# One stationary block for the rounded values and their rest in the 64-column heads, and the two halves of the bank added afterwards

## What is computed

```python
o_a = _diff_attention(a_q, a_k, a_v, ...)        # 4 heads, values 128 wide, then a norm per head
o_b = _forgetting_attention(b_q, b_k, b_v, ...)  # 8 heads, values 64 wide
o_c = _stick_breaking_attention(c_q, c_k, c_v)   # 8 heads, values 64 wide
m = (gates[:, :, 0] * (o_a @ proj_a[l])
     + gates[:, :, 1] * (o_b @ proj_b[l])
     + gates[:, :, 2] * (o_c @ proj_c[l]))
h = h + m @ w_out[l]
```

## Time and profile before

| | us |
|---|---|
| executions | 2615.31, 2614.27, 2615.72 |
| median | 2615.31 |
| profiled execution, device time | 2615.27 |
| its span | 2613.5 |
| TensorE busy | 2579.9 |
| VectorE busy | 1429.5 |
| ScalarE busy | 1104.7 |
| granted TensorE clock | 0.998 of full speed |

### The profile page before, as it was taken

The page is one execution under the profiler, slowest core; times in us unless marked ns, Lnnn a source line. Parts: engine busy times, 40 slices in busy tenths (PEclk is TensorE's granted clock), DMA queues, the critical chain, the costliest instruction groups (busy, mean ns, idle before and its releaser), DMA issues.

```text
span 2613.5 us, 37200 instructions
## 1 busy us (share of the span) xinstructions
PE 2579.9 (99%) x11966; PEld 2142.6 (82%) x11966; DVE 1429.5 (55%) x2260; ACT 1104.7 (42%) x1856; POOL 7.0 (0%) x13
## 2 busy tenths in 40 slices
PE   7999999999999999999999999999999999999998
PEld 6888888888888888888888888888888888888886
DVE  5444347788854464444344443477787455544434
ACT  4333237776632243332233322477776223433322
POOL 0000000000000000000000000000000000000000
PEclk9999999999999999999999999999999999999999
DMA  4222331111122232222332222211111222322232
GB/s 166 96 96 97 103 106 57 65 58 57 57 90 97 95 113 96 96 96 102 108 105 96 96 97 105 89 65 60 62 57 57 100 93 95 115 96 96 97 105 104
DMA packets 65769, 238.07 MB, mean 91 GB/s; under 512 B 7296, under 2 KB 7552, under 8 KB 65408
## 3 DMA queue, kind: packets, MB, share of 16 engines
q1 hardware_dynamic: 65664, 236.79, 26.0%
HBM read 234.66 MB, written 2.10 MB: 91 GB/s over the span
## 4 chain that ended last, share of the span: by engine, by line
PE 91%; DVE 4%; ACT 2%; issue 2%; DMA 0%; DVEq 0%; ACTq 0%; SPq 0%
PE ps L372 29%; PE ps L374 28%; PE ps L373 28%; PE ps L504 2%; ACT area L738 2%; DVE stat L1166 1%; DVE w_lo L1030 1%; PE ps L454 1%; DVE area L1030 1%; PE ps L443 0%; PE ps L445 0%; PE ps L491 0%; PE ps L493 0%; DVE area L1160 0%; DVE scratch L1046 0%
## 5 line engine op out<-in xcount | busy, mean ns | idle before, releaser
L738 ACT ACTIVATE w_hi<-w_raw 128x1024 fp32r<-128x1024 f32 x441 | 468.6, 1063 | 1161.1 <-PE ps L374 1160.2
L372 PE MATMUL ps<-u_hi,w_hi 128*128 128x512 f32 x2368 | 928.6, 392 | 13.9 <-DVE w_lo L1030 13.5
L374 PE MATMUL ps<-u_hi,w_lo 128*128 128x512 f32 x2368 | 923.0, 390 | 0.0
L373 PE MATMUL ps<-u_lo,w_hi 128*128 128x512 f32 x2368 | 922.9, 390 | 0.0
L1030 DVE TENSOR_TENSOR w_lo<-w_raw,w_hi 128x1024 fp32r<-128x1024 f32 x441 | 538.9, 1222 | 313.8 <-ACT w_hi L738 305.7
L372 PEld LDWEIGHTS ps<-u_hi,w_hi 128*128 128x128 f32 x2368 | 445.2, 188 | 105.7 <-issue 13.1
L374 PEld LDWEIGHTS ps<-u_hi,w_lo 128*128 128x128 f32 x2368 | 445.1, 188 | 93.8
L373 PEld LDWEIGHTS ps<-u_lo,w_hi 128*128 128x128 f32 x2368 | 445.4, 188 | 90.8 <-issue 1.0
L372 PE MATMUL ps<-area,w_hi 128*128 128x512 f32 x1024 | 398.8, 389 | 0.4 <-DVE h L1050 0.4
L374 PE MATMUL ps<-area,w_lo 128*128 128x512 f32 x1024 | 398.4, 389 | 0.0
L373 PE MATMUL ps<-area,w_hi 128*128 128x512 f32 x1024 | 398.4, 389 | 0.0
(11 more groups left out here) (112 smaller groups left out, 1621.8 us busy)
## 6 DMA issues: line engine op xcount, KB each, us to landing
w_raw<-weights SPq DMA_DIRECT2D x441, 512.0 KB, 3.2
h<-x SPq DMA_DIRECT2D x2, 1024.0 KB, 7.3
out<-scratch SPq DMA_DIRECT2D x8, 256.0 KB, 2.2
scratch<-const_b SPq DMA_DIRECT2D x1, 512.0 KB, 10.7
scratch<-const_r SPq DMA_DIRECT2D x1, 320.0 KB, 10.3
scratch<-lambdas SPq DMA_DIRECT2D x1, 256.0 KB, 11.3
cst<-const SPq DMA_DIRECT2D x1, 137.0 KB, 2.2
par<-params SPq DMA_DIRECT2D x1, 94.0 KB, 2.0
```

Source lines behind the costliest of these rows:

```text
L372: pe.matmul(dst, hi, x_hi, start=start, stop=False, **kw)
L373: pe.matmul(dst, hi, x_lo, start=False, stop=False, **kw)
L374: return pe.matmul(dst, lo, x_hi, start=False, stop=stop, **kw)
L738: return act.activation(dst, src, ACT.Copy)
```

## The change

The values of a 64-column head are put into one block of 128 columns: head 0's rounded values on columns 0 to 63 and their rest on 64 to 127, head 1's the other way round. `val(branch, hd)` is now such a pair of one head, not a part of both; there are no zeros, and `v_area` shrinks from 4096 to 3072 columns, with GpSimd's fill and the wait for it gone. A head's sum is two matmuls per block of keys (with the rounded and with the rest weights), both with the same stationary block. The product of the two rests is in it now, which was left out before. Half of the bank then holds what the rounded values give, the other half what their rest gives, and the two have to be added:

- `output_rest(hd)` on ScalarE copies the half of the rest, across the partitions, into `o_rest` at the head's own half;
- `output_whole(hd)` on VectorE adds the bank's other half to it, into `o_whole`;
- `output_hi` and `output_lo` of these branches read `o_whole` (SBUF), not the bank.

Each head is an accumulation group of its own, so the bank is free for the next one only when `output_whole` of the last has run; the TensorE waits for that (`o_whole_set`) ahead of each sum. `weighted_whole` keeps the three matmuls for the differential branch. In the stick-breaking output's place `values_hi(1)` and `values_lo(1)` with `rows` now go ahead of `output_hi(2, t)` and `output_lo(2, t, layer)`.

```diff
@@ val, val_block
-            at = j * P if branch == 0 else j * 3 * HEAD + head * HEAD
-            return val(branch, part)[:, at:at + P]
+        def val_block(branch, part, j):
+            return val(branch, part)[:, j * P:(j + 1) * P]
...
-            pool.memset(v_area[:].bitcast(F32), 0.0).then_inc(zeros_set, 1)
...
+            def weighted(branch, hd):
+                for j in range(NQ):
+                    pe.wait_ge(pt_set, c.next(pt_set))
+                    n, w_hi_j, w_lo_j = wide_keys(j)
+                    v = val_block(branch, hd, j)
+                    pe.matmul(ps[:, OB, SEQ - n:SEQ], v, w_hi_j, start=j == 0, stop=False)
+                    last = pe.matmul(ps[:, OB, SEQ - n:SEQ], v, w_lo_j, start=False, stop=j == NQ - 1)
+                last.then_inc(o_mm, 1)
...
-                weighted(1, 1, False, True)
+                pe.wait_ge(o_whole_set, c.next(o_whole_set))
+                weighted(1, 1)
...
-            at = 2 * hd * HEAD
-            return val(branch, part).rearrange("p (j e) -> p j e", j=NQ)[:, :, at:at + HEAD]
+            at = HEAD * (hd ^ part)
+            return val(branch, hd).rearrange("p (j e) -> p j e", j=NQ)[:, :, at:at + HEAD]
...
-                    act.wait_ge(o_mm, c.next(o_mm))
-                    hi(area[:, bass.ds(at, SEQ)], ps[:, OB, :]).then_inc(o_hi_set, 1)
+                    act.wait_ge(o_whole_set, c.next(o_whole_set, 2))
+                    hi(area[:, bass.ds(at, SEQ)], o_whole[:]).then_inc(o_hi_set, 1)
+
+            def output_rest(hd):
+
+                act.wait_ge(o_mm, c.next(o_mm))
+                act.activation(o_rest[half(hd), :], ps[half(1 - hd), OB, :], ACT.Copy).then_inc(o_rest_set, 1)
...
@@ ScalarE, rest_of_tile
                 split(0)
+                output_rest(1)
                 c.skip(score_set, NQ)
                 exps(0)
                 output_hi(1, t - 1)
...
@@ ScalarE, heads
                 qk_hi(1, 0, 3)
+                output_rest(0)
                 stick_logs()
...
                 split(0)
+                output_rest(1)
                 c.skip(score_set, NQ)
                 exps(0)
+                values_hi(1)
                 output_hi(2, t)
-                values_hi(1)
                 split(1)
...
                 split(2)
+                output_rest(0)
                 c.skip(score_set, NQ)
                 exps(1)
...
+            def output_whole(hd):
+
+                dve.wait_ge(o_rest_set, c.next(o_rest_set))
+                dve.tensor_tensor(o_whole[half(hd), :], ps[half(hd), OB, :], o_rest[half(hd), :], ALU.add
+                                  ).then_inc(o_whole_set, 1)
...
@@ VectorE, rest_of_tile
                 softmax(0, vec_done)
+                output_whole(1)
                 output_lo(1, t - 1, layer)
                 difference(layer)
...
@@ VectorE, heads
                 qk_lo(1, 0, 3)
+                output_whole(0)
                 stick_softplus()
...
                 softmax(0, prob_set)
+                output_whole(1)
+                rows(t * 2 + 1, 1, 1)
+                values_lo(1)
                 output_lo(2, t, layer)
-                values_lo(1)
-                rows(t * 2 + 1, 1, 1)
                 stage(7, 1.0)
...
                 softmax(1, prob_set)
+                output_whole(0)
                 for hd in range(2):
                     rows(t + N_FOX, 0, hd)
```

More of the change, by code:

```diff
@@ L164, in trunk @@
         v_area = sb("v_area", V_COLS, F32R)
+        o_rest = sb("o_rest", SEQ)
+        o_whole = sb("o_whole", SEQ)
         scratch = sb("scratch", 8 * SEQ)
@@ L216, in val @@
         def val(branch, part):
-            at = V_AT[branch] + part * (V_AT[branch + 1] - V_AT[branch]) // 2
-            return v_area[:, at:at + (V_AT[branch + 1] - V_AT[branch]) // 2]
-        def val_block(branch, head, part, j):
-            at = j * P if branch == 0 else j * 3 * HEAD + head * HEAD
-            return val(branch, part)[:, at:at + P]
+            at = (2 * branch + part) * SEQ
+            return v_area[:, at:at + SEQ]
+        def val_block(branch, part, j):
+            return val(branch, part)[:, j * P:(j + 1) * P]
         def tile(k):
@@ L467, in wide_keys, with weighted_whole @@
                 return n, area[:, PT_HI + end - n:PT_HI + end], area[:, PT_LO + end - n:PT_LO + end]
[L469 to L473, removed]
+            def weighted_whole():
+                pe.wait_ge(v_set, c.next(v_set))
+                pe.wait_ge(o_whole_set, c.next(o_whole_set))
                 for j in range(NQ):
                     pe.wait_ge(pt_set, c.next(pt_set))
-                    v_hi, v_lo = (val_block(branch, head, p, j) for p in range(2))
                     n, w_hi_j, w_lo_j = wide_keys(j)
[L478 to L481, removed]
+                    last = three(ps[:, OB, SEQ - n:SEQ], val_block(0, 0, j), val_block(0, 1, j), w_hi_j, w_lo_j,
+                                 start=j == 0, stop=j == NQ - 1)
+                last.then_inc(o_mm, 1)
[6 more added lines that the diff above has]
+                    last = pe.matmul(ps[:, OB, SEQ - n:SEQ], v, w_lo_j, start=False, stop=j == NQ - 1)
+                last.then_inc(o_mm, 1)
             def stick_scores(hd):
@@ L555, in heads @@
                 if before:
-                    weighted(0, 0, True, True)
+                    weighted_whole()
                 unit(3, 3, 5)
@@ L573, in heads @@
                 unit(5, 0, 3)
-                weighted(2, 0, True, False)
+                pe.wait_ge(v_set, c.next(v_set))
+                if before:
+                    pe.wait_ge(o_norm, c.next(o_norm))
+                weighted(2, 0)
                 stick_scores(1)
@@ L582, in heads @@
                 unit(7, 0, 4)
-                weighted(2, 1, False, True)
+                pe.wait_ge(o_whole_set, c.next(o_whole_set))
+                weighted(2, 1)
                 pe.wait_ge(rows_set, c.next(rows_set))
@@ L592, in heads @@
                 unit(8, 2)
-                weighted(1, 0, True, False)
+                pe.wait_ge(v_set, c.next(v_set))
+                pe.wait_ge(o_whole_set, c.next(o_whole_set))
+                weighted(1, 0)
                 pe.wait_ge(rows_set, c.next(rows_set))
@@ L1232, in output_lo @@
                 at = (t + branch * NT) * SEQ
-                src = ps[:, OB, :]
+                src = o_whole[:]
                 if branch == 0:
```

22 lines of the change are left out of this document (12 added, 10 removed).

## The result

| | before | after |
|---|---|---|
| median of the runs, us | 2614.89 (6 runs, 2614.27 to 2615.72) | 2626.11 (6 runs, 2624.79 to 2627.72) |
| profiled execution, us | 2615.27 | 2626.04 |
| its span, us | 2613.5 | 2624.2 |
| TensorE busy | 2579.9 | 2572.3 |
| VectorE busy | 1429.5 | 1453.4 |

The ratio is 1.0043, 95% interval 1.0030 to 1.0056. The forecast was 2623.6, with a range of 2614 to 2630: right in sign and in kind, and 2.5 us short. Of the change itself, 8.3 us were forecast and 11.2 measured.

A forecast was written before the change was run, and what follows sets the result against it. TensorE bounds the stick half, VectorE and ScalarE the softmax half (transposes to differential sum). Per layer 3 x 2.44 + 1.98 - 4 x 1.29 = +4.14, two layers +8.3: 2615.3 + 8.3 = 2623.6 us, range 2614 to 2630.

The forecast's parts named there:

- Stick half: Tile from the differential sum to the next transposes: two heads' savings count in full, nothing added shows, -1.29 us per tile.
- Rival (d): Stick half loses too: ScalarE's copy ahead of the logs delays the stick sums by the matmuls' saving; 2633.9 us, 6%.
- Steps 1 to 4: Softmax half, tile start to the next softmax: forgetting head 1's sum slips +1.11 us, the next first maximum +0.93.
- step 1: Tile start: stick-breaking head 1's add waits for the scaling's end (0.12 us); the turned weights' rounding slips 0.51.
- Step 2: After the turned rounding: ScalarE runs without a gap and VectorE follows it into the next softmax, all +0.51 us.
- Step 5: Forgetting head 1's output: VectorE adds, ScalarE rounds, VectorE waits, then takes the rest; next maximum +2.44 us.
- Step 6: Second softmax to the differential sum: turned rest and sum slip the same 2.44 us; the transposes have cover enough.
- The last half: Last softmax half of a layer: VectorE waits 0.66 us for scores there, so TensorE's saving counts; +1.98 us.
- (a): All cover holds: adds fall into idle time and every removed matmul counts, 20.6 us less, 2594.7 us; 6%.
- (b): Softmax half keeps its length while the stick half saves 10.3 us: 2605.0 us; 7%.
- (c): Break-even: Step 5's round trip costs half, net slip 1.3 us per softmax half against 1.29 saved, 2615.3 us; 11%.
- (e): Weighted sums: the change does not take twelve matmuls to eight as it says; no size or chance given.

The follow-up runs named there:

- e1: Changed kernel with VectorE taking the forgetting output's rest behind difference and stage(1), add and rounding left in place: 2614.08 us.
- e3: Changed kernel with the rest-weights matmul made twice, so twelve matmuls per 64-column head again, copies and adds kept: 2639.05 us.
- e7: Changed kernel with a second o_whole; forgetting head 1's add, its rounding, both outputs' rests and (except last halves) the differential values' rest moved later: 2603.69 us.
- e6: Changed kernel with the moves of e1 and e2, plus the differential values' rest moved to VectorE idle time except in last halves: 2606.86 us.
- e4: Changed kernel with eight matmuls per head but no copy and no add, output rounded straight from the bank with the old waits: 2602.85 us.
- e2: Changed kernel with ScalarE rounding the weight unit (split(1)) ahead of the stick-breaking output: 2622.92 us.

## Why the prediction was right, and where it was off

**Stick half, right to 0.02.** Said -1.29 per tile, measured -1.31 (49.88 to 48.57). The copy ahead of the stick logs pushes what comes of them, as said, and there is cover:

```profile
590.79 1.70 DVE L1058 TENSOR_TENSOR area<-scratch,area 128x512 fp32r<-128x512 f32 x4
...
593.53 2.98 PE L513 MATMUL ps<-area,cst_r 128*128 128x512 f32 x20
```

The rest of the stick weights is done at 592.49, 1.04 ahead of the stick sums (2.12 before, said 0.9). The stick sums come 29.71 after the differential sum (593.53 - 563.82) instead of 30.37, 0.66 earlier. Rival (d) is out. The tile as a whole takes 81.43 (525.75 to 607.18), said 81.4.

**Steps 1 to 4, right in mechanism, 0.15 too dear.** The add behind the scaling on partitions 64 to 127 came 0.52 after its start (525.33 - 524.81), the one on 0 to 63 0.40 after (541.31 - 540.91): the hold cost the 0.12 that step 1 gave it. The turned rounding slipped by 0.50 (527.54 + 0.96 - 528.00; said 0.51). Step 2 had all of it carried on, and the chain did not: the first maximum of the next softmax slipped 0.48 and its last scaling 0.36 (540.91 + 0.96 - 541.51), because that softmax had 0.11 to spare ahead of its 512-column maximum. What comes from that is 0.15 less further on: turned rest and sum of head 1 +0.95 (said +1.11), next maximum at 546.87, +0.78 (said +0.93).

**Step 5, right.** Said +2.44 for the first maximum of `difference`, measured +2.38; the round trip alone is 1.60 against the 1.51 said. The difference is at its end: the next maximum starts 0.72 after the rest (553.95 - 553.23), and the sum had taken over the 0.61 of before (552.53 - 551.92). e1 took the trip away and gave back 1.34 to 1.47 in each of the first three halves.

**Step 6, right in what slipped, wrong on the transposes.** The differential sum slipped 2.39 (said 2.44). The transposes ahead of it, which were to have cover enough, wait 0.56 themselves (560.25). Over the first three turns of layer 0 the halves grew by 2.17, 2.39 and 2.75, in the mean 2.44. That this mean is the forecast to the hundredth is luck. VectorE has idle times of about 0.3 us that no releaser explains, and they lie at other places in the two kernels. The first line is the kernel before, the second the changed one in its third half:

```profile
467.02 0.42 DVE L1166 TENSOR_REDUCE stat<-ps 128x1 f32<-128x256 f32 x1 [0.30 <-PE ps L445]
...
636.83 0.21 DVE L1221 TENSOR_SCALAR stat<-stat,lam 128x1 f32<-128x1 f32 x1 [0.28 <-DVE stat L1219]
```

The scores that the first reads were written by 466.44, and the reciprocal ahead of the second ended at 636.55. In both kernels the idle time comes again at the same place in layer 1 (1757.45 and 1931.63). The first half of before is 0.33 longer by it, the third of the changed kernel 0.25. Without them the halves grew by 2.50, 2.39 and 2.50. Why the times lie where they lie stays open.

**The last half, mis-sized.** Said +1.98, measured +2.35 in layer 0. The term from TensorE held: the first maximum behind the gate units stands at 709.50 against 707.53, and that, less the 1.55 of its tile, is +0.42 (said 0.47). What was missed is in the softmax behind it:

```profile
709.50 0.29 DVE L1194 TENSOR_REDUCE stat<-ps 128x1 f32<-128x128 f32 x1
...
710.83 0.16 DVE L1205 RECIPROCAL stat<-stat 128x1 f32<-128x1 f32 x1 [0.30 <-ACT scratch L851]
...
714.81 0.69 DVE L1274 TENSOR_TENSOR o_whole<-ps,o_rest 64x512 f32<-64x512 f32 x1
716.20 0.69 DVE L1058 TENSOR_TENSOR area<-o_whole,area 128x512 fp32r<-128x512 f32 x1 [0.70 <-ACT area L758]
```

The reciprocal waits 0.30 that it did not wait before, at the same place in both layers. ScalarE's sum that it needs was written at 710.47, 0.36 ahead of its start, where 0.03 is what the same pair took before (708.51 and 708.54). So the releaser named does not explain it: it is an idle time of the same kind, worth 0.33, and the other 0.09 is step 5's. With the third half's 0.25 such times make 1.2 us in the softmax halves of the changed kernel, and 0.7 in those of the kernel before; on balance they add some 0.5 us to the measured difference. Their cause stays open.

**What the sum had no term for: the clock.** From the first weighted sum to the last, layer 0's mixer grew 4.45 and layer 1's 5.70 (said 4.14 each). The 1.3 between the two are in layer 1's last softmax half, 32.54 against 31.24. The TensorE's timelines of the same stretch, layer 0 and then layer 1:

```profile
722.11 0.55 PE L454 MATMUL ps<-cst,scratch 128*128 128x128 f32 x3 [1.36 <-DVE scratch L1224]
723.22 0.66 PE L454 MATMUL ps<-cst,scratch 128*128 128x128 f32 x4 [0.56 <-DVE scratch L1224]
723.63 0.47 PE L372 MATMUL ps<-u_hi,w_hi 128*128 128x512 f32 x1
...
724.17 0.40 PE L374 MATMUL ps<-u_hi,w_lo 128*128 128x512 f32 x1
724.41 0.40 PE L372 MATMUL ps<-u_hi,w_hi 128*128 128x512 f32 x1
```

```profile
2016.94 0.55 PE L454 MATMUL ps<-cst,scratch 128*128 128x128 f32 x3 [1.36 <-DVE scratch L1224]
2018.05 0.98 PE L454 MATMUL ps<-cst,scratch 128*128 128x128 f32 x4 [0.56 <-DVE scratch L1224]
...
2019.68 0.63 PE L374 MATMUL ps<-u_hi,w_lo 128*128 128x512 f32 x1
2020.11 0.63 PE L372 MATMUL ps<-u_hi,w_hi 128*128 128x512 f32 x1
```

The waits are the same, but the matmuls after them start 0.43 apart in layer 1 and 0.23 in layer 0. The stretches of both, and of the end of the kernel (us, busy time of TensorE, its weight loads, VectorE, ScalarE, GpSimd, granted clock, DMA):

```profile
723.00:727.00 4.00, 3.75 (x20) 3.02 (x21) 2.98 (x6) 1.43 (x4) 0.00 (x0) 1.00 0.37 119
...
2018.50:2022.50 4.00, 4.00 (x14) 3.29 (x13) 2.31 (x5) 1.43 (x4) 0.00 (x0) 0.61 0.40 131
...
2612.00:2618.00 6.00, 2.07 (x2) 0.50 (x2) 3.68 (x6) 2.21 (x3) 0.00 (x0) 0.51 0.02 9
```

The granted clock fell from 2.4 GHz to its lower level, 1.2, for some 3 us after those waits. The last 0.95 us is at the end of the kernel, in the final norm behind a TensorE wait of 3.53 us, where the two matmuls of the sum of squares take 2.07 us at that level against 1.12 before:

```profile
2612.72 2.07 PE L393 MATMUL ps<-scratch,cst 128*128 128x512 f32 x2 [3.53 <-DVE scratch L1074]
```

Before had the same 3.53 us wait there, and a clock of 0.60 from 2603 to 2608, where the two matmuls lie at 2602.91; so what differs is when the fall comes, not that it comes. All nine traces have this wait. The two matmuls take 1.12 or 1.13 us in the kernel before, e3 and e7 and 2.07 or 2.08 in the other six. e7 has the eight matmuls and the adds as the changed kernel has, so the change alone does not make this term.

Together: 4.45 + 5.70 + 0.95, less 0.5 that the changed kernel was ahead at the first weighted sum, is 10.6 of the 10.7 by which the spans differ. The 0.5 is scatter: that sum starts between 419.38 and 420.39 in the nine traces, and e6, which has the change, is the latest. The sum of the prediction had 8.3 for the mixers; without the fallen clock they made 8.9.

**The hold.** Behind the start of the same scaling of 0.49 us the two adds on partitions 64 to 127 start 0.52 later (525.33 and 551.84), that is behind its end, and the one on partitions 0 to 63 starts 0.40 later (541.31), ahead of its end. The Trainium skill, page "VectorE: DVE Perf Modes", section "Two Vector instructions with no wait between them", has the rule that an instruction whose start quadrant (a group of 32 partitions) is another than that of the one ahead waits for all those ahead of it to finish; the trace of the changed kernel agrees (0.52 against 0.40).

**The rivals.** (a), 2594.7 with every saving counted, was further off than it looked: even e4, with no adds at all, stops at 2602.85. (b), a softmax half that keeps its length, is not what the change did (32.99 against 30.56); it is what e7 reaches (30.21 against 30.56), but only with the adds in idle time; its 2605.0 and e7's 2603.69 are close. (c) needed a round trip of half its price, and it took its full one (1.60). (e) is out: 128 matmuls are gone, four for each of 32 heads.

## What to carry to other kernels

Where a fast engine is busy 99% of the time, its work still has two prices: full in the stretches where it never waits, and about a sixth in those where another engine keeps pace with it (1.30 and 0.21 us for the same matmuls, put back into the changed kernel). Before work is shifted from it to the others, find which stretches pay, and place the new work in idle time of the receiving engines by name; the same adds cost 23 us in one order (some 1.3 of it by the clock that fell behind them) and, with one other rest moved as well, about 1 us in another. The dearest form is a result that goes from VectorE to ScalarE and back while VectorE has nothing else in its list: give the intermediate a buffer of its own and take its last step later.

## What was not expected of the hardware

The granted clock of the TensorE fell in one of two equal places. The pair of waits of 1.36 and 0.56 us ahead of the last transposes is in both layers of the changed kernel. In the changed kernel and in e2 the half behind it is longer in layer 1 (by 1.30 and 1.17 us), in e3 in layer 0 (by 1.15), and in e1 and e4 to e7, which have no wait over 0.6 us at these transposes, in neither. That the waits make such a fall possible is likely from that, not shown; what decides between two equal places stays open. A slip of VectorE can thus cost more than its length, by about half as much again when the clock falls behind it.
